# Expert gate and up weights loaded as 8 KB runs per partition, with token transposes that read every eighth column

## What is computed

```python
def expert_block(args):
    xi, e = args
    hid = jax.nn.silu(xi @ w_gate[e]) * (xi @ w_up[e])
    return hid @ w_down[e]
```

## Time and profile before

| | us |
|---|---|
| median of 3 runs | 1873.25 |
| lowest and highest run | 1869.59, 1873.69 |
| span of the profiled execution | 1870.0 |
| TensorE busy in that span | 1523.7 (81%) |
| TensorE weight loads busy | 946.7 (51%) |
| VectorE busy | 530.3 (28%) |
| DMA, mean over the span | 285 GB/s |

### The profile page before, as it was taken

One profiled execution on the slowest core, in us unless ns is written; L12 is line 12 of the kernel. 1 busy time (PEld: TensorE's weight loads), 2 busy tenths in 40 slices (PEclk: granted clock), 3 DMA queues, 4 the chain that ended last, 5 costly groups with the idle time before them and its releaser, 6 DMA issues.

```text
span 1870.0 us, 23688 instructions
## 1 busy us (share of the span) xinstructions
PE 1523.7 (81%) x8676; PEld 946.7 (51%) x8676; DVE 530.3 (28%) x1000; ACT 160.4 (9%) x321; POOL 242.0 (13%) x380
## 2 busy tenths in 40 slices
PE   5987898889999679888778788778778788787773
PEld 3664676557777566445435445434435345343331
DVE  6768777677300530100000100100100100010006
ACT  3011111101300110000000000000000000000001
POOL 3537544440000110000000000000000000000004
PEclk9998999889999879999999999999999899999997
DMA  6795455452398249999999999999999999999984
GB/s 166 170 212 132 114 118 130 118 122 90 95 275 263 70 152 352 331 380 392 375 381 392 377 380 390 380 381 391 386 368 390 379 375 388 382 385 390 394 290 151
DMA packets 330370, 533.41 MB, mean 285 GB/s; under 512 B 26368, under 2 KB 174944, under 8 KB 309536
## 3 DMA queue, kind: packets, MB, share of 16 engines
q1 hardware_dynamic: 313504, 487.80, 74.2%
q0 software_dynamic: 3712, 27.26, 6.3%
q10 hardware_dynamic: 13120, 17.90, 3.2%
HBM read 498.91 MB, written 34.01 MB: 285 GB/s over the span
## 4 chain that ended last, share of the span: by engine, by line
PE 42%; DMA 32%; DVE 11%; SPq 10%; issue 4%; POOL 1%; ACT 0%; DVEq 0%; ACTq 0%; POOLq 0%
DMA e_ring<-in_w_exp_up_dram 24%; PE bank L978 19%; PE bank L1268 7%; PE bank L1286 6%; SPq L551 5%; SPq L578 5%; DMA e_ring<-in_w_exp_gate_dram 3%; DMA w_ring<-in_w_in_dram 2%; DVE e_ring L1470 2%; PE bank L1199 2%; PE bank L1252 2%; PE bank L1129 2%; PE bank L1020 1%; DMA e_ring<-in_w_exp_down_dram 1%; DVE e_ring L1474 1%
## 5 line engine op out<-in xcount | busy, mean ns | idle before, releaser
L1268 PE MATMUL bank<-e_ring,xT_exp 128*64 128x256 f32 x4096 | 507.2, 398 | 166.0 <-DMA e_ring<-in_w_exp_gate_dram 101.0
L1268 PEld LDWEIGHTS bank<-e_ring,xT_exp 128*64 128x64 f32 x4096 | 290.8, 142 | 394.6 <-DMA e_ring<-in_w_exp_gate_dram 147.6
L978 PE MATMUL bank<-xT,w_ring 128*128 128x288 f32 x1024 | 267.5, 421 | 5.7 <-DMA w_ring<-in_w_in_dram 5.0
L1286 PE MATMUL bank<-e_ring,hidT 128*64 128x512 f32 x1024 | 234.4, 605 | 43.5 <-DMA e_ring<-in_w_exp_down_dram 27.0
L978 PEld LDWEIGHTS bank<-xT,w_ring 128*128 128x128 f32 x1024 | 199.3, 197 | 67.9 <-issue 7.9
L978 PE MATMUL bank<-hT,w_ring 128*128 128x288 f32 x896 | 221.9, 409 | 0.0
L1744 DVE TENSOR_TENSOR hid<-bank,sig_exp 128x256 f32<-128x256 f32 x32 | 13.6, 424 | 659.2 <-ACT sig_exp L929 659.2
L978 PEld LDWEIGHTS bank<-hT,w_ring 128*128 128x128 f32 x896 | 170.3, 191 | 46.2
L1286 PEld LDWEIGHTS bank<-e_ring,hidT 128*64 128x64 f32 x1024 | 69.6, 137 | 185.4 <-issue 113.9
L725 POOL DMA_INDIRECT e_ring<-expert_rows_out,idx x6 | 5.5, 925 | 1136.5 <-ACT all_stored_mark L754 1135.0
L1755 DVE COPY rows<-bank 128x512 f32<-128x512 f32 x32 | 22.1, 691 | 253.9 <-PE bank L1286 253.9
(11 more groups left out here) (298 smaller groups left out, 1126.7 us busy)
## 6 DMA issues: line engine op xcount, KB each, us to landing
e_ring<-in_w_exp_gate_dram SPq DMA_DIRECT2D x128, 1024.0 KB, 14.6
e_ring<-in_w_exp_up_dram SPq DMA_DIRECT2D x128, 1024.0 KB, 14.4
e_ring<-in_w_exp_down_dram SPq DMA_DIRECT2D x128, 1024.0 KB, 15.4
w_ring<-in_w_in_dram SPq DMA_DIRECT2D x32, 1024.0 KB, 6.2
expert_rows_out<-hT POOLq DMA_DIRECT2D x11, 1536.0 KB, 12.2
w_ring<-in_w_out_dram SPq DMA_DIRECT2D x16, 1024.0 KB, 7.6
w_ring<-in_w_ple_gate_dram SPq DMA_DIRECT2D x16, 1024.0 KB, 21.0
w_ring<-in_ssm_w_glu_dram SPq DMA_DIRECT2D x4, 1024.0 KB, 4.8
```

The source lines that it names most:

```text
L978: last_mm = pe.matmul(out, weights(k), moving[:, k, :], start=(k == 0), stop=(k == n - 1))
L1268: mm = pe.matmul(gu[h * B:(h + 1) * B, s % 2, :], xT_exp[:, k % 8, k // 8, :], w[:, kk, h * FH:(h + 1) * FH], start=(s == 0 and kk == 0), ...
L1286: mm = pe.matmul(bank[h * B:(h + 1) * B, 3 + n, :], hidT[:, j % 2, j // 2, :], e_ring[:, 8 + j, h * DH2 + n * 512:h * DH2 + (n + 1) * 512] ...
```

## The change

The contraction rows of the gate and up matrices are dealt to partitions in another order. A half of the matrix (h, 1024 rows) is cut into 128 groups of 8 neighbouring rows, and partition p holds rows 8p to 8p+7 of the half. One piece takes 4 of the 8 rows (c0 is 0 or 4), so a partition's piece is one run of 4 x 2 KB = 8 KB in DRAM, and neighbouring partitions start 16 KB apart. Number, size and order of the pieces, the slots and the waits stay as they are.

The tokens must be dealt in the same way: block c of `xT_exp` holds in partition p column 8p + c of the half. So the transpose of block c reads every eighth column of `x_exp`, beginning at c, where it read 128 neighbouring columns. The matmuls and their operands in `xT_exp` are unchanged in number, shape and place; the sum over the 2048 rows is taken in another order.

```diff
@@ -112,8 +112,8 @@
-    wg_v = w_exp_gate[0].rearrange("e (k p) f -> p e k f", p=P)
-    wu_v = w_exp_up[0].rearrange("e (k p) f -> p e k f", p=P)
+    RUN = D // 2 // P
+    wg_v, wu_v = (w[0].rearrange("e (h p c) f -> p e h c f", h=2, c=RUN) for w in (w_exp_gate, w_exp_up))
     wd_v = w_exp_down[0].rearrange("e (j p) n -> p e j n", p=P)
@@ -543,7 +543,8 @@
                 if s < 8:
-                    src = (wg_v, wu_v)[s % 2][:, ds(e, 1), 4 * (s // 2):4 * (s // 2) + 4, :]
+                    c0 = 4 * (s // 2 % 2)
+                    src = (wg_v, wu_v)[s % 2][:, ds(e, 1), s // 4, c0:c0 + 4, :]
                     dst = e_ring[:, s, :].rearrange("p (a k f) -> p a k f", a=1, k=4)
@@ -1249,7 +1250,8 @@
                 for c in range(KC // 2):
-                    mm = pe.transpose(bank[:, 1 + c // 4, (c % 4) * P:(c % 4 + 1) * P], x_exp[:, c * P:(c + 1) * P], ident[:])
+                    mm = pe.transpose(bank[:, 1 + c // 4, (c % 4) * P:(c % 4 + 1) * P],
+                                      x_exp.rearrange("r (p c) -> r c p", c=RUN)[:, c, :], ident[:])
                 mm.then_inc(xeT_ready, 1)
```

## The result

The changed kernel takes 1819.59 us (median of 4 runs, 1818.36 to 1826.44), the kernel before beside it 1873.47 us (1869.59 to 1876.54). The ratio is 0.9723, 95% interval 0.9702 to 0.9745: 54 us or 2.8% faster, where 1820 us had been forecast. The profiled span is 1816.7 us against 1870.0 us.

The account below looks back on a forecast made before the run. The prediction took the rate of the DMA engines to bound experts 2 to 31. 1870.0 - 55 (loads) + 3 (transposes) = 1818 us of span, the median 3 us above it, put at 1820 us; range 1802 to 1850 us.

Parts of the forecast that it names:

- The bound and its bounds in time: Experts 2 to 31 stand in a DMA-bound stretch of 1060 us, from 753.31 to 1813.35 us; the rest is untouched.
- The price of a piece: Gate and up pieces take 2.48 us like down pieces, not 2.71: 0.23 us each, 55 us over 30 experts.
- The spread over DRAM: Gate and up runs lying 16 KB apart cost nothing; at most 0.23 us a piece.
- Rival 1: Gate and up loads: packet form is only part of the gap, 28 us gained, 1845 to 1848 us; chance 0.12 with other partial gains.
- Rival 2: Gate and up loads get no faster, pieces still at 2.7 us: 1870 to 1877 us; chance 0.05.
- The transposes: Strided weight loads at L1252 add 1 us a turn; three uncovered turns cost +3 us, bounds 0 to +7.
- the prediction's lower bound: Transposes' weight load at L1252 stays as long as now, cost 0, since nothing makes a wider stride faster.
- Rival 3: Strided weight load at L1252 makes TensorE the bound and the kernel slower, about 1950 us at 10 us a turn; chance 0.06.
- the account: Nine-times turns, forecast for that run: a pair needs 57.5 + 16 = 73.5 us of TensorE, 6.1 more than the DMA.
- What is late next: Even to odd half of a pair: TensorE comes level, 30.5 us against 29.8 for the pieces, but DMA still binds.

Follow-up runs that it names:

- e5: The changed kernel with every turn of 8 token transposes made five times: 1837.80 us.
- e8: The changed kernel with SP's embedding loads of a pair moved from before the even expert's first piece to behind its fourth: 1816.12 us.
- e4: The changed kernel with 8 KB runs 8 KB apart instead of 16 KB, a piece being one closed MB, transposes reading every fourth column: 1818.49 us.
- e3: The changed kernel with two runs of 4 KB per partition and piece instead of one of 8 KB, transposes reading every second column: 1835.41 us.
- e1: The kernel before with the strided transposes alone, its loads still in 2 KB runs: 1872.58 us.
- e6: The changed kernel with every turn of 8 token transposes made nine times: 1919.70 us.
- e2: The changed kernel with the old transposes of neighbouring columns, so the 8 KB loads alone: 1823.86 us.

## Why the prediction was right

**The bound and its bounds in time.** The DMA-bound stretch was to begin behind SP's wait for expert 1's `ple_proj` and to end with the last down piece. SP of the changed kernel, in order of time:

```profile
749.81 0.39 SPq L579 DMA_DIRECT2D w_ring<-in_w_ple_proj_dram  x1
750.53 0.34 SPq L552 DMA_DIRECT2D e_ring<-in_w_exp_gate_dram  x1
```

It begins 2.8 us earlier than in the earlier trace rows, no later; the first turn had begun 3.2 us earlier too (698.8 against 702.0), which is the drift of the stages before. From the first turn to SP's first piece of the stream it is 51.7 us now and was 51.3: the three turns that were to cost 3 us there cost about 0.4. e5 and e8 show the two sides of this bound: TensorE's work inside the stretch is covered, and an earlier start of the stream is kept for the most part.

**The price of a piece.** The down pieces had been taken as the price of the new form, 2.48 us, and 2.48 us it is. 240 pieces x 0.23 us made 55 us; 51.5 us were measured over the experts, 0.215 us a piece. By the turns, the 24 experts of the twelve pairs from expert 4 on took 853.3 us before and 811.2 after, 1.75 us less each, 0.22 us a piece; the last four took 134.3 and 128.2, only 1.5 us less each; the first four give the remaining 3.3 us. So the price, read from a single gap, was 0.01 us too high for the pairs, which makes 2 to 3 us, and the rest is missing at the two ends. Why a piece gained less there was not looked into.

**The spread over DRAM.** Taken at nothing; e4, with the same length of the experts within 0.1 us, shows nothing of it. Rival 1 falls with it: e4 has no spread and no more gain, and e3 lies where the length of the run puts it. Rival 2 falls by the windows, 416 to 419 GB/s at a share of 1.00 to 1.01.

**The transposes.** This term was mis-sized, though within its bounds. It had +1 us a turn and +3 us in all; the turn grew by 0.07 us, and e1 says 0.0 us for the whole. The turn had been taken to double; its weight loads did become longer, by 53 ns each, but most of that is hidden behind the transposes. The overestimate of 3 us and the overestimate of the gain by 3.5 us cancel, which is why 1820 meets 1819.59 so closely; the drift of the early stages alone is larger than that difference.
The Trainium skill (page "SBUF — State Buffer", section "Door 1: The DMA port swizzle") counts a stride of up to 4 fp32 as free. The traces of e3 and e4 disagree: a step of 2 already has the whole cost, 209 ns against 140, a step of 4 has 211 ns, and a step of 8 no more than that, 193 ns. That last figure also goes against the prediction's lower bound, which held that nothing makes a wider stride faster.

**Rival 3, TensorE as the bound.** The mechanism is real and was placed right: e6 shows it, and its pair of 73.9 us is near the 73.5 us of the account (57.5 + 16). Part of that is luck: the repeated turns took 0.88 instead of 1 us, which makes 71.6 us, and TensorE was busy for only 69.05 of the pair's 73.9 us. Of the 4.8 us left it spent 3.8 waiting for pieces of the queue that had run empty and 1.0 waiting for `hidT`, and the account had neither. Its busy time was below the account's 71.6 us at a granted clock of 1.00 (from 813 to 1700 us in e5 and e6), where the 57.5 us had been taken from pairs at 0.97 to 0.98. The slowdown came at 7 us more per turn, where the change added 0.07.

**What is late next.** TensorE was to come level with the DMA in the even to odd half. In the changed kernel, TensorE in order of time after an even expert's turn at 1181.1 us, with the odd expert's pieces:

```profile
1190.77 7.09 PE L1288 MATMUL bank<-e_ring,hidT 128*64 128x512 f32 x32 [0.52 <-DVE hidT L1751]
1197.69 10.53 PE L1270 MATMUL bank<-e_ring,xT_exp 128*64 128x256 f32 x96
1208.63 1.95 PE L1270 MATMUL bank<-e_ring,xT_exp 128*64 128x256 f32 x16 [0.41 <-DMA e_ring<-in_w_exp_gate_dram]
1211.12 1.95 PE L1270 MATMUL bank<-e_ring,xT_exp 128*64 128x256 f32 x16 [0.54 <-DMA e_ring<-in_w_exp_up_dram]
```

Six pieces are used without a wait, and the last two are waited for, by half a us each: nearly level. In the mean over the pairs from expert 4 on this half fell from 33.7 to 31.9 us and the other from 37.6 to 35.7, so both still took their share of this gain. It should follow that a further one is taken in the odd to even half alone; no run tests that.

## What to carry to other kernels

Where a stage is bound by its weight loads, look for two forms of transfer of one size side by side in the trace, and compare the GB/s of windows that hold only one of them: that gave the price of the longer run before anything was built, to within 0.01 to 0.02 us a piece. A contraction dimension can be dealt to the partitions in any order as long as both operands are dealt alike, so that neighbouring rows can make one long run; the strided read that this put on the tokens' transposes cost 0.07 us for a turn of 8 here. Then count how much room the engine that is not the bound still has in each round of the loop, and look for the waits of the queue's issuer on it: in e6 the slowdown began at such a wait.

## What was not expected of the hardware

- The time from issue to landing nearly doubled, 14.4 to 14.6 us before and 27.1 to 27.3 us after, in a kernel that is faster. Of gate pieces between 800 and 1700 us SP's issue lasted 2.3 us in the median before and 1.2 after, of up pieces 2.3 and 0.35 us. With a quarter of the packets per piece more pieces are in flight and SP is held up less: 27.2 us at one piece each 2.48 us are 11 pieces, nearly all of the 12 slots, so after the change the ring itself comes to be the limit. Before it was 5 (14.5 at 2.71), and in e3, with half the packets, 7 (19.0 us at 2.56). So fewer packets let more be queued, but half the packets did not let twice as many pieces in, and what the limit is stays open. The longer landing time cost nothing, so it says nothing of the rate.
- A weight load of 128 fp32 columns took 140 ns for neighbouring columns and 209, 211 and 193 ns for a step of 2, 4 and 8. The widest step was the cheapest of the three; why is not shown.
- With equal work the stages before the experts end anywhere in 9 us (698.3 to 707.0 us), and from the last turn to the end it took 64.0 to 69.5 us in the nine traces with single turns, while the experts of the changed kernel repeated within 0.1 us in the end and 0.8 us along the way. A difference of 4 us between medians can lie outside the part that was changed, as in e2.
- TensorE's granted clock rose when it was given more to do: from 813 to 1700 us it was busy 748 us at a mean granted clock of 0.96 in the changed kernel, and 810 us at 1.00 in e5.
